# Attention with the value products directly behind a burst of scores

## The chip, the cores and the metric

The kernel runs on one core of one Trainium2 chip. The metric is the device time of one execution, in microseconds (us). Three executions of the kernel before took 730.85, 731.18 and 731.60 us; the median is 731.18 us.

## The reference, cut to what matters

The program is one layer of an encoder with 1024 tokens of 1024 features in float32: RMS norm, one input projection, three token mixers, output projection with residual, then RMS norm and a mixture of 32 experts, and a last norm. The change concerns two of the mixers, the attentions:

```python
def neighbourhood_attention(q, k, v, rel_bias):      # 4 heads of 64
    s = jnp.einsum('bhcd,bhrcjd->bhcrj', q_r, k_r).astype(jnp.float32) + bias
    p = jax.nn.softmax(s.reshape(B, H, GRID_W, kr * NA_COLS), axis=-1)
    return jnp.einsum('bhcrj,bhrcjd->bhcd', p, v_r)
...
def sliding_window_gqa(q, k, v, sink):               # 8 query heads, 2 key/value heads
    s = jnp.einsum('bnqgrd,bnkgd->bngrqk', qb, kb).astype(jnp.float32)
    s = jnp.where(jnp.asarray(valid)[None, :, None, None], s + alibi, -jnp.inf)
    p = jax.nn.softmax(jnp.concatenate([s, sink_logit], axis=-1), axis=-1)[..., :-1].astype(v.dtype)
    o = jnp.einsum('bngrqk,bnkgd->bnqgrd', p, vb)
```

Each query block of 128 tokens looks at its own key block and the ones before and after it: 384 keys, or 256 for the first and the last block.

## The kernel before, in words

The attention stage lies between the input projection and the output projection. It has 24 steps, made by `attention_plan` (line 89 on). Steps 0 to 7 are the neighbourhood attention of one query block each, with four heads. Steps 8 to 23 are the sliding-window attention, two steps for each query block, one for each key/value head (g = 0, then g = 1), with four query heads in each. So every step has four units u = 4s to 4s+3, one for each head, and 96 units in all.

What happens to a unit:

- TensorE multiplies query and key into one of four PSUM banks (`scores`, lines 801 to 816). The bank is u modulo 4, so the score of unit u waits until the evaluation of unit u-4 is done (`bias_done`).
- DVE evaluates the bank (`bias_and_max`, line 1505): it adds bias or distance, takes the row's extreme and writes the unit to SBUF. Line 1514 is the neighbourhood form, line 1526 the sliding-window form; the latter has a small copy of the sink in front of each step's first unit (line 1523).
- ACT takes the exponential and the row sum (line 1177). DVE takes the reciprocal of the sum two units later (line 1533). The normalisation is DVE's for some units (line 1550) and POOL's for the others (line 2039).

When all four units of a step are normalised, TensorE transposes them in chunks of 128 keys, four transposes to a chunk (`transposes`, line 829). A step has three chunks, or two at the edges. There are three PSUM banks for chunks, and DVE or ACT copies each to SBUF (`evacuate_chunk`, lines 485 and 490), by a rule that goes by the chunk's number. The value products (`times_values`, line 847 for the neighbourhood, line 853 for the sliding window) use the copied chunks. In the sliding window they come once for two steps, since the products of both key/value heads fill one bank. ACT copies that bank out (line 1190).

The order is written out by the plan as a list of ticks. Tick u carries the scores' units: at each u that is a multiple of four TensorE issues all four scores of a step as a burst, and then what the tick lists. An entry T is one chunk's transposes, an entry V one chunk's value products. The softmax of a step runs 8 ticks ahead of its first chunk (`lag = 8`), so that the chunks of step s begin in tick 4s+11, one tick in front of the scores of step s+3.

DVE and ACT walk through the same ticks in order. In each tick DVE does the evaluation of unit u, the reciprocal and, where it is DVE's, the normalisation of unit u-2, and then the evacuations of this tick's T entries that are its own. From tick 98 on it also splits the first output weights. ACT does the exponential of unit u, the copy of a finished value bank whose last V stood in the tick before, and then its own evacuations of the tick. An instruction that waits holds up all that is behind it on its engine. POOL only normalises, unit by unit.

In the plan before, a step's list is: its three T, then the V of the step before (where there is one), spread evenly over four ticks. For a step with three chunks and a V of three this gives T T | T | V V | V, and the burst of scores opens the second of these four ticks, so that TensorE runs: T, T, scores, T, V, V, V. For a sliding-window step without a V it is T | T | T.

After the last value products the output projection begins (lines 891 to 893), and later the experts, whose weights SyncE fetches as products release their buffers.

Of the kernel before, what the change touches and what calls it, by code (L numbers as in the profile page):

```python
# [61 lines left out]
MAGIC = 12582912.0  # L62

MIX_FROM = 8
GROUP = 3
LAST_QUERIES = (4, 8)
SLOPES = tuple(2.0 ** -(h + 1) for h in range(SWA_HEADS))
POOL_LAG = 2
# [20 lines left out]
def attention_plan():  # L89


    steps = []
    for i in range(TT):
        lo, hi = max(i - 1, 0), min(i + 2, TT)
        steps.append(("na", i, 0, lo * P, (hi - lo) * P))
    for b in range(TT):
        lo, hi = max(b - 1, 0), min(b + 2, TT)
        for g in range(SWA_KV):
            steps.append(("swa", b, g, lo * P, (hi - lo) * P))
    lag = 8  # L100
    ticks = [[] for _ in range(4 * len(steps) + lag + 4)]
    late = []
    for s, (kind, i, g, k0, nk) in enumerate(steps):
        nc_ = -(-nk // P)
        items = []
        for c0 in range(0, nc_, GROUP):
            group = range(c0, min(c0 + GROUP, nc_))
            items += [("T", s, c) for c in group]
            items += late
            late = [("V", s, c) for c in group] if kind == "na" or g == 1 else []  # L110
        if s == len(steps) - 1:
            items += late
        for j, it in enumerate(items):
            ticks[4 * s + 3 + lag + (4 * j) // len(items)].append(it)
    return steps, ticks


def encoder(nc, x, norm1_g, w_in, nat_tab, swa_sink, pool_w, pool_scale, w_out, norm2_g,
            rg_w, rg_b, re_w, re_b, e_gate, e_up, e_down, final_g,
            c_sq, c_namask, c_alibi, c_iedge, c_misc, c_dest, out):  # L120
    steps, ticks = attention_plan()
    NU = 4 * len(steps)

# [2062 lines left out]
```

How the kernel before makes its waits and increments, by code:

```python
        def chunk_ready(eng, n):  # L408
            if n >= 0:
                mine = by_vector(n)
                eng.wait_ge(pt_v if mine else pt_a, sum(by_vector(m) == mine for m in range(n + 1)))
# [63 lines left out]
        def evacuate_chunk(eng, copy, done, s, c):  # L476
            n = chunk_no[(s, c)]
            kind, i, g, k0, nk = steps[s]
            w = min(P, nk - c * P)
            eng.wait_ge(tr_done, n + 1)
            if kind == "na":
                if s >= 2:
                    eng.wait_ge(pv_done, vnum[(s - 2, last_chunk[s - 2])] + 1)
                copy(ptna[s % 2][0:w, c, :], ps[0:w, tbank(n), :]).then_inc(done, 1)
            else:
                before = NA_STEPS - 2 + i if i < 2 else NA_STEPS + 2 * (i - 2) + 1
                eng.wait_ge(pv_done, vnum[(before, last_chunk[before])] + 1)
                copy(ptswa[i % 2][c][:, g, :], ps[:, tbank(n), :]).then_inc(done, 1)
# [2 lines left out]
        @block.sync  # L493
# [1 line left out]
            def load_x(t):  # L495
                if t >= NX:
                    sp.wait_ge(x_in[t % NX], 16)
                sp.dma_start(xin[t][:], x[0, t * P:(t + 1) * P, :]).then_inc(x_in[t % NX], 16)
# [1 line left out]
            def load_w(i):  # L500
                m = ORDER[i]
                if i >= 2:
                    sp.wait_ge(w_split, 2 * (i - 1))
                sp.dma_start(wraw[i % 2][:], w_in[0, :, m * P:(m + 1) * P].rearrange("(k p) n -> p k n", p=P)
                             ).then_inc(w_in_s[i % 2], 16)
# [101 lines left out]
            sp.wait_ge(out_mm, TT)
            fetch_expert(0)
```

## Time and profile before

| | us |
|---|---|
| median of three runs | 731.18 |
| the profiled execution | 730.85 |
| its span, first to last instruction | 729.0 |
| TensorE busy in the span | 704.2 |
| VectorE (DVE) busy | 508.0 |
| ScalarE (ACT) busy | 390.1 |
| GpSimd (POOL) busy | 321.8 |

The span's times count from the first instruction. A busy TensorE is modelled from its pipelined matmuls, so the idle time in front of its weight loads (PEld) says more. A float32 transpose or matmul shows as two records, so a chunk of four transposes has eight, and the trace may group or miss some of them. Scores of two heads run side by side on the two halves of the array's rows, and the two key/value heads' products on the two halves of its columns, which is why their records come in pairs with the same start.

### The profile page before, as it was taken

Reading aid. Unit: us, or ns where it says so; the run is one execution under the profiler, and the core shown is the slowest. Engines: PE = TensorE matmul, PEld = TensorE weight load, DVE = VectorE, ACT = ScalarE, POOL = GpSimd, SP = SyncE. Lnnn points to the kernel's source line nnn. Section 1 sums busy time; section 2 is a strip of 40 time slices with the busy share of each in tenths; the row PEclk is TensorE's granted clock in tenths of the full one; section 3 lists DMA queues with packets and bytes.
Section 4 is the critical chain, followed back from the end, with each engine's and each line's share of the span. In section 5 each row is a group of like instructions: output and inputs, shape, how many; then the busy total and the mean of one; then the engine's idle time right before and its main releaser. Section 6 shows DMA issues by size and latency. Waiting matters only on the chain.

```text
span 729.0 us, 10252 instructions
## 1 busy us (share of the span) xinstructions
PE 704.2 (97%) x3757; PEld 511.3 (70%) x3757; DVE 508.0 (70%) x811; ACT 390.1 (54%) x585; POOL 321.8 (44%) x241
## 2 busy tenths in 40 slices
PE   7999999999999999999999899999999999999983
PEld 6888888886775556888889666666666666666631
DVE  5646422215988887214377898888888888888977
ACT  6500000104888887001122688888888888887815
POOL 2423458953778771610000454444444444442213
PEclk9999999999999999999999999999999999999997
DMA  9422112100400003705666599999999999999978
GB/s 308 140 58 58 32 55 59 30 0 23 123 1 1 1 1 140 206 5 200 230 227 207 178 351 385 390 384 381 383 383 384 390 383 383 385 386 379 400 273 350
DMA packets 62419, 157.74 MB, mean 216 GB/s; under 512 B 10168, under 2 KB 24992, under 8 KB 62368
## 3 DMA queue, kind: packets, MB, share of 16 engines
q1 hardware_dynamic: 55728, 139.58, 52.9%
q0 software_dynamic: 6336, 16.89, 7.0%
q8 instruction: 31, 0.51, 0.3%
q10 hardware_dynamic: 304, 0.59, 0.2%
q14 instruction: 20, 0.16, 0.1%
HBM read 142.36 MB, written 18.87 MB: 221 GB/s over the span
## 4 chain that ended last, share of the span: by engine, by line
PE 88%; DMA 5%; DVE 3%; SPq 1%; issue 1%; ACT 1%; POOL 0%; DVEq 0%; POOLq 0%
PE ps L1008 7%; PE ps L1013 7%; PE ps L1016 7%; PE ps L727 6%; PE ps L725 6%; PE ps L726 6%; PE ps L829 4%; PE ps L891 4%; PE ps L893 4%; PE ps L892 4%; PE ps L1039 4%; PE ps L1043 4%; PE ps L1035 4%; PE ps L814 3%; DMA wd<-in_expert_w_down 3%; PE ps L853 3%
## 5 line engine op out<-in xcount | busy, mean ns | idle before, releaser
L1810 DVE TENSOR_TENSOR wgulo<-wgu,unit 128x2048 fp32r<-128x2048 f32 x64 | 146.2, 2286 | 26.4 <-ACT unit L1276 26.4
L1276 ACT CAST unit<-wgu 128x2048 fp32r<-128x2048 f32 x64 | 122.2, 1910 | 3.7 <-PE ps L949 1.6
L2084 POOL DMA_INDIRECT expert_rows<-ysb,idx x32 | 70.8, 2212 | 108.2 <-ACT ysb L1323 107.2
L2077 POOL DMA_INDIRECT xg<-h_rows,idx x32 | 59.2, 1849 | 71.2 <-PE ps L984 58.3
L725 PE MATMUL ps<-hThi,whi 128*128 128x512 f32 x200 | 78.3, 392 | 0.0
L727 PE MATMUL ps<-hThi,wlo 128*128 128x512 f32 x200 | 77.9, 389 | 0.0
L726 PE MATMUL ps<-hTlo,whi 128*128 128x512 f32 x200 | 77.8, 389 | 0.0
L1816 DVE TENSOR_TENSOR wdlo<-wd,unit 128x2048 fp32r<-128x2048 f32 x32 | 73.1, 2285 | 2.6 <-ACT unit L1285 2.5
L1008 PE MATMUL ps<-unit,xThi 128*80 128x512 f32 x256 | 70.9, 398 | 0.8 <-ACT xThi L1300 0.8
L1013 PE MATMUL ps<-unit,xTlo 128*80 128x512 f32 x256 | 69.2, 391 | 0.0
L1016 PE MATMUL ps<-wgulo,xThi 128*80 128x512 f32 x256 | 69.1, 391 | 0.0
L1285 ACT CAST unit<-wd 128x2048 fp32r<-128x2048 f32 x32 | 61.1, 1909 | 4.8 <-DMA wd<-in_expert_w_down 4.8
L2039 POOL TENSOR_SCALAR pswa<-pswa,esum 128x384 f32<-128x384 f32 (+1 forms) x48 | 55.9, 1182 | 12.8 <-DVE esum L1533 12.8
L1137 ACT COPY kb<-ps 64x512 f32<-64x512 f32 x8 | 4.7, 583 | 92.6 <-DVE ps L1410 92.5
L1013 PEld LDWEIGHTS ps<-unit,xTlo 128*80 128x80 f32 x256 | 37.8, 148 | 21.1 <-DVE xTlo L1823 0.2
L1016 PEld LDWEIGHTS ps<-wgulo,xThi 128*80 128x80 f32 x256 | 37.8, 148 | 21.1
L891 PE MATMUL ps<-wohi,oThi 128*128 128x512 f32 x128 | 51.3, 401 | 0.0
L893 PE MATMUL ps<-wohi,oTlo 128*128 128x512 f32 x128 | 50.0, 391 | 0.0
L892 PE MATMUL ps<-wolo,oThi 128*128 128x512 f32 x128 | 49.9, 390 | 0.0
L1008 PEld LDWEIGHTS ps<-unit,xThi 128*80 128x80 f32 x256 | 35.4, 149 | 16.7 <-ACT xThi L1300 0.9
L1177 ACT ACTIVATE pswa<-pswa,mneg 128x385 f32<-128x385 f32 (+1 forms) x64 | 37.6, 588 | 13.0 <-DVE mneg L1526 12.8
L1972 POOL TENSOR_SCALAR stat<-stat 128x1 f32<-128x1 f32 x16 | 5.5, 344 | 87.8 <-ACT h L1249 65.3
(226 smaller groups left out, 1449.4 us busy)
## 6 DMA issues: line engine op xcount, KB each, us to landing
wgu<-in_expert_w_gate SPq DMA_DIRECT2D x64, 512.0 KB, 12.4
wgu<-in_expert_w_up SPq DMA_DIRECT2D x64, 512.0 KB, 15.3
wd<-in_expert_w_down SPq DMA_DIRECT2D x32, 1024.0 KB, 17.5
y<-expert_rows SPq DMA_DIRECT2D x16, 512.0 KB, 9.8
wraw<-in_w_in SPq DMA_DIRECT2D x14, 512.0 KB, 3.9
xin<-in_x SPq DMA_DIRECT2D x8, 512.0 KB, 6.7
x<-in_x SPq DMA_DIRECT2D x8, 512.0 KB, 7.3
out<-fo SPq DMA_DIRECT2D x8, 512.0 KB, 3.3
```

Source lines behind the costliest of these rows:

```text
L725: nc.tensor.matmul(bank, whi[i % 2][:, k, :], hThi[:, k, cols], start=(k == 0), stop=False)
L726: nc.tensor.matmul(bank, whi[i % 2][:, k, :], hTlo[:, k, cols], start=False, stop=False)
L727: mm = nc.tensor.matmul(bank, wlo[i % 2][:, k, :], hThi[:, k, cols], start=False, stop=(k == KT - 1))
L891: nc.tensor.matmul(ps[:, g % 4, :], oThi[t][:, k, :], wohi[n][:, k, :], start=(k == 0), stop=False)
L892: nc.tensor.matmul(ps[:, g % 4, :], oThi[t][:, k, :], wolo[n][:, k, :], start=False, stop=False)
L893: mm = nc.tensor.matmul(ps[:, g % 4, :], oTlo[t][:, k, :], wohi[n][:, k, :], start=False, stop=(k == KT - 1))
L1008: nc.tensor.matmul(bank, xThi[e % 2][:, 4 * a + k, :], hi[:, :, k * DE:(k + 1) * DE], start=(a == 0 and k == 0), stop=False)
L1013: nc.tensor.matmul(bank, xTlo[e % 2][:, 4 * a + k, :], hi[:, :, k * DE:(k + 1) * DE], start=False, stop=False)
L1016: mm = nc.tensor.matmul(bank, xThi[e % 2][:, 4 * a + k, :], lo[:, :, k * DE:(k + 1) * DE], start=False, stop=(a == 1 and k == 3))
L1276: nc.scalar.copy(weight_unit(e, a)[:], raw_half(wgu, e, a)).then_inc(ahi_done, 1)
L1810: nc.vector.tensor_tensor(raw_half(wgulo, e, a), raw_half(wgu, e, a), weight_unit(e, a)[:].bitcast(F32), ALU.subtract).then_inc(alo_done, 1)
L1816: nc.vector.tensor_tensor(wdlo[e % RING][:].rearrange("p j d -> p (j d)").rearrange("p (a f) -> p a f", a=2), wd[e % RING][:].rearrange("p ...
```

## The change

The plan no longer spreads a step's list evenly. With first = 4s+11, a step's chunks stand in ticks first, first+2 and first+3, and the V of the step before stands as a whole in tick first+1, the tick of a burst of scores. TensorE then runs: T, scores, V, V, V, T, T. The constant `GROUP`, which was 3 and so never split a step's chunks, is gone. The numbers of the chunks, and with them their banks and the engine that evacuates each, stay as they were, and so do the waits.

```diff
-        items = []
-        for c0 in range(0, nc_, GROUP):
-            group = range(c0, min(c0 + GROUP, nc_))
-            items += [("T", s, c) for c in group]
-            items += late
-            late = [("V", s, c) for c in group] if kind == "na" or g == 1 else []
+        first = 4 * s + 3 + lag
+        ticks[first + 1] += late
+        for c in range(nc_):
+            ticks[first + (0, 2, 3)[c]].append(("T", s, c))
+        late = [("V", s, c) for c in range(nc_)] if kind == "na" or g == 1 else []
         if s == len(steps) - 1:
-            items += late
-        for j, it in enumerate(items):
-            ticks[4 * s + 3 + lag + (4 * j) // len(items)].append(it)
+            ticks[first + 3] += late
```

## Rows read from the trace of the kernel before

**Rows 1.** The page's first line.
```profile
span 729.0 us, 10252 instructions
```
**Rows 2.** Table by stretch: length, busy time of each engine, granted clock, DMA share, GB/s.
```profile
178.40:283.00 104.60, 103.68 (x707) 61.54 (x705) 88.18 (x344) 83.55 (x238) 76.41 (x65) 1.00 0.09 26
...
400.00:700.00 300.00, 295.52 (x1540) 198.70 (x1539) 267.50 (x225) 240.06 (x226) 129.04 (x63) 1.00 0.99 367
393.00:397.00 4.00, 4.00 (x29) 4.00 (x29) 3.23 (x18) 2.44 (x2) 0.00 (x0) 0.57 0.98 379
```
**Rows 3.** TensorE's weight loads in order of time, neighbourhood steps: start, us, what.
```profile
185.73 0.42 PEld L829 LDWEIGHTS ps<-ident,pna 128*128 128x128 f32 x4 [0.55 <-issue]
...
188.37 0.95 PEld L809 LDWEIGHTS ps<-ka,qa 64*128 64x128 f32 x8 [0.17 <-issue]
189.86 0.42 PEld L829 LDWEIGHTS ps<-ident,pna 128*128 128x128 f32 x4 [0.54 <-DVE ptna L485]
190.45 1.29 PEld L847 LDWEIGHTS ps<-ptna,vtok 128*64 128x64 f32 x24 [0.17 <-issue]
191.91 0.86 PEld L829 LDWEIGHTS ps<-ident,pna 128*128 128x128 f32 x8 [0.17 <-POOL pna L2039]
192.93 0.95 PEld L809 LDWEIGHTS ps<-ka,qa 64*128 64x128 f32 x8 [0.17 <-issue]
...
211.38 1.29 PEld L847 LDWEIGHTS ps<-ptna,vtok 128*64 128x64 f32 x24 [0.55 <-issue]
```
**Rows 4.** DVE in order of time, neighbourhood steps.
```profile
192.60 0.69 DVE L485 COPY ptna<-ps 128x512 f32<-128x512 f32 x1 [0.16 <-PE ps L829]
193.88 0.56 DVE L1514 CUSTOM_DVE_ANT_0 pna<-ps,ti 128x384 f32<-128x384 f32 x1 [0.58 <-PE ps L809]
...
198.43 0.41 DVE L1514 CUSTOM_DVE_ANT_0 pna<-ps,te 128x256 f32<-128x256 f32 x1
```
**Rows 5.** TensorE's weight loads in order of time, one pair of sliding-window steps.
```profile
243.85 0.42 PEld L829 LDWEIGHTS ps<-ident,pswa 128*128 128x128 f32 x4 [0.81 <-POOL pswa L2039]
244.44 0.95 PEld L814 LDWEIGHTS ps<-kb,qs 64*128 64x128 f32 x8 [0.17 <-issue]
245.93 1.29 PEld L829 LDWEIGHTS ps<-ident,pswa 128*128 128x128 f32 x12 [0.55 <-issue]
...
247.99 0.30 PEld L814 LDWEIGHTS ps<-kb,qs 64*128 64x128 f32 x4 [0.17 <-DVE mneg L1526]
248.53 0.40 PEld L814 LDWEIGHTS ps<-kb,qs 64*128 64x128 f32 x2 [0.24 <-DVE mneg L1526]
249.13 0.29 PEld L814 LDWEIGHTS ps<-kb,qs 64*128 64x128 f32 x2 [0.20 <-DVE mneg L1526]
249.97 0.42 PEld L829 LDWEIGHTS ps<-ident,pswa 128*128 128x128 f32 x4 [0.54 <-issue]
250.56 0.20 PEld L853 LDWEIGHTS ps<-ptswa,vtok 128*64 128x64 f32 x4 [0.17 <-issue]
...
253.29 0.42 PEld L829 LDWEIGHTS ps<-ident,pswa 128*128 128x128 f32 x4 [0.81 <-POOL pswa L2039]
```
**Rows 6.** DVE in order of time, the same pair.
```profile
246.33 0.42 DVE L1550 TENSOR_SCALAR pswa<-pswa,esum 128x384 f32<-128x384 f32 x1
...
247.87 0.60 DVE L1526 CUSTOM_DVE_ANT_0 pswa<-ps,dist,nsink 128x384 f32<-128x384 f32 x1
...
248.47 0.60 DVE L1526 CUSTOM_DVE_ANT_0 pswa<-ps,dist,nsink 128x384 f32<-128x384 f32 x1
...
251.25 0.70 DVE L1550 TENSOR_SCALAR pswa<-pswa,esum 128x384 f32<-128x384 f32 x1
```
**Rows 7.** TensorE's weight loads, the end of the attention stage.
```profile
281.11 0.20 PEld L853 LDWEIGHTS ps<-ptswa,vtok 128*64 128x64 f32 x4 [0.48 <-ACT ptswa L490]
...
282.97 0.19 PEld L891 LDWEIGHTS ps<-wohi,oThi 128*128 128x128 f32 x1 [0.81 <-issue]
```
**Rows 8.** The chain of waits in order of time, expert stage.
```profile
647.99 21.75 DMA wd<-in_expert_w_down
```

More of the change, by code:

```diff
@@ L64 @@
 MIX_FROM = 8
-GROUP = 3
 LAST_QUERIES = (4, 8)
```

## The prediction

> **What bounds the kernel now.** I read the page first (span 729.0 us, [rows 1]), then the table by stage. In the attention stage, 178.4 to 283 us, TensorE is busy for 103.68 of 104.60 us, DVE for 88.18, and the DMA engines are almost idle; from 400 to 700 us the DMA share is 0.99 [rows 2]. TensorE's figure is modelled, so I went on to its weight loads in order of time, which show where it stands still, and to DVE in the same stretch. The chain of waits was read last, to see whether time lost in attention can be won back later.
>
> Names: S is a step's burst of four scores, T one transposed chunk (four transposes), V a step's value products. b is DVE's evaluation of one score bank, n its normalisation, ev the evacuation of a transposed chunk. Of the four scores in S, the first two wait for the first two b of the step before, the third for the third b, the fourth for the fourth.
>
> Neighbourhood steps: S starts at 188.37, T at 189.86 (1.49 us later), V at 190.45 (0.59), two T at 191.91 (1.46), next S at 192.93 (1.02) [rows 3]. A step is 4.56 us, nothing but TensorE's work. DVE is only slightly ahead: it stands 0.58 us before one b [rows 4].
>
> Sliding-window steps in pairs: T, S, four T, S, T, V, T, from 243.85 to 253.29, so 9.44 us: 0.59 + 1.49 + 2.06 + 1.98 + 0.59 + 2.73 [rows 5]. The first S runs freely in 1.49. The second does not: its third and fourth score wait for DVE (248.53 and 249.13), right behind the third and fourth b of the first S, which DVE finishes at 248.47 and 249.07 [rows 5, 6]. So in each pair TensorE is the bound, except in one burst, where DVE is.
>
> **What the change does to TensorE's own time.** No instruction is added or dropped, and no DMA is moved. A T between two other kinds takes 0.59, each further one in a row 0.43: two are 1.02 [rows 3], three 1.45. V behind S costs no more than V behind T: at 211.38 V follows 1.49 behind S and takes 1.46 [rows 3]. A neighbourhood step becomes 1.49 + 1.46 + 1.45 = 4.40, 0.16 less. A pair becomes, with its second S still at 1.98, 1.49 + 1.45 + 1.98 + 2.73 + 1.45 = 9.10, 0.34 less. If TensorE were alone, that would be the result.
>
> The trace's shapes change at each kind (scores 64*128, transposes 128*128, values 128*64), and the dearer first T is seen there. The Trainium skill, TensorEngine Tiling (Array Packing), Key Properties, says that changing the tiling mode drains the engine. By that rule fewer changes of kind mean a shorter stage; 0.16 us a change is what the rows show, and it is rival 1.
>
> **What it does to DVE.** DVE works in order. Its ev of a chunk stands in the tick where TensorE's T stands, behind that tick's b. In a step with V, the second T was before V, or before the burst; now it stands behind V, and its ev stands in front of the third b (a chunk that DVE takes as the step's third: in front of the fourth b). DVE therefore waits until S, V and T are over, with b's queued behind it for which the next S waits. DVE can begin ev 0.69 after the start of T (191.91 to 192.60) [rows 3, 4].
>
> A pair, with the start of its first S as 0. I take DVE's times from the row at 244.44. Steady state: T(s,1) behind V is at -1.45; its ev runs from -0.73 to -0.05; third and fourth b, 0.60 each [rows 6], end at 0.5 and 1.1. The third score starts at 0.57, the fourth at 1.17. A lone last score keeps TensorE for 0.84 (249.13 to 249.97) [rows 5], so T begins at 2.01 instead of 1.49. Three T last to 3.46, the second S starts. DVE goes on with the sink copy at 1.03, b to 1.87, n (0.42), b, ev (0.69), b to 4.11, b to 4.72: 0.1 later than now. The fourth score starts at 4.78, V at 5.62, T at 8.35, the next S at 9.80. I take 9.77 with the small overlaps of the rows: **+0.33 us a pair**. The T moved out of the half where TensorE waited for DVE anyway into the one where nothing is idle, and the free burst is now throttled too.
>
> Neighbourhood steps. b is 0.54 to 0.56, ev 0.69 [rows 4]. S4 still ends at 185.73 [rows 3]; V0 (1.02), three T and S5 follow, which starts at 188.20, 0.17 earlier than now. V1 starts at 189.92, T(2,1) at 191.38, its ev 192.1 to 192.8, third and fourth b to 193.76. S6 starts at 192.83, its fourth score at 193.82 instead of 193.36, V2 at 194.66. Laid out on in this way, the starts of S against now are: S6 -0.10, S7 +0.08, S8 +0.37, S9 +0.48, S10 +0.68 us. About +0.2 a step, where TensorE alone would give -0.16. The bursts of 256 columns (S7 to S9) have b of 0.41 [rows 4] to 0.48, which is in these numbers.
>
> Between the kinds: the chunk T(7,1) and then the first sliding chunks move behind V as well. Same method: S11 +1.31, S12 +1.15, S14 +1.68, S15 +1.13, S16 **+1.63**. Then three pairs to S22: +1.0. The last bursts and V19 have 256 columns and give back 0.4: V19 **+2.26**.
>
> Tail. Before, seven T stand behind V19; now nine, as T(20,1) and T(20,2) come behind it: 0.86. The pooled products wait for the last b, which is behind an ev: about 0.26. V23 waits now for ACT's ev of T(23,0) (0.48 before 281.11) and goes on to the output projection at 282.97 [rows 7]; that chain moves as it is. **+1.12**.
>
> ACT and POOL: ACT's copy of V's output now stands before the third exponential instead of behind the fourth, and waits for the end of V, 3.05 us into a neighbourhood step. The third b is at 4.1 or later in the steps where DVE waits, and its reciprocal comes two ticks on, so I take nothing. POOL's normalisations end 4 us before the T that needs them. Bounds: nothing to 0.3 us a step, over the five neighbourhood steps 0 to 1.5. DVE's n is 0.42 at 246.33 and 0.70 at 251.25 [rows 6]. The n in the path of the second S is the 0.42; should it come out as 0.70, a pair costs 0.28 more, over four pairs 1.1.
>
> Sum: 2.26 + 1.12 = **+3.4 us**. The profiled execution took 730.85 us, 1.85 around its span of 729.0; it would take 734.25. The median is 731.18, so **734.6**. Can it be won back? From 400 us the DMA engines are full, but their fetches are released by TensorE's products: the chain holds a 21.75 us transfer at 648 us that was issued behind TensorE's own work [rows 8]. The whole train starts later. TensorE's clock: from 393 to 397 us it was granted 0.57 on average, with the half level of 1.2 GHz in most of it, while the router's small products ran [rows 2]. Where that dip falls after a shift I can't say; its work takes 4 us, so at most half of it, and I allow 1 us either way.
>
> **Rivals.**
> 1. Faster: TensorE's changes of kind decide. 0.16 on six neighbourhood steps and 0.34 on six pairs, 3.0 us: 728.2. For it: TensorE is busy 99% of the stage. Against: the third and fourth score start 0.06 behind DVE's b already [rows 5, 6], and DVE has 88 of 104.6 us of work [rows 2] and would now stand over 1 us in each V step. It decides if ev behind V ends before the next S needs the third b, that is if DVE's wait were under 0.5 us. 9%.
> 2. Gains and waits cancel: the first free steps gain 0.16 each, the tail's waits are covered by output work: about +1 us, 732.2. 7%.
> 3. The later stages swallow it, since the expert stage is DMA bound: 731.2. Against: [rows 8], fetches are released by products. 4%.
> 4. More than that: ACT's early copy delays exponentials, or n takes 0.70. 2.6 us on top: 737.2. 12%.
> 5. The forecast, 734.6, own range 732.7 to 736. 68%.
>
> What this kernel's measurement can tell from no change is about 0.2%, 1.5 us. Slower 80%, same 11%, faster 9%. The range for 8 in 10 is 731.5 to 737.0: from rival 3's edge, over rival 2, to nearly the whole of rival 4.
>
> **What the profile after would show.** In a pair: V directly behind the second S; DVE idle for about 1 us before ev of line 490, released by TensorE's line 829; both bursts broken into single scores released by DVE; a pair of 9.7 to 9.8. In the neighbourhood steps the same idle before line 485, steps of 4.6 to 4.8. First output projection at 286.3 instead of 282.97, with everything behind it moved by as much. I am wrong if bursts stay at 1.49 and pairs fall under 9.3 (rival 1), or if DVE's waits are there but the last burst isn't later, or if the shift is gone at 400 us (rival 3).

## The result, and the profile after

The changed kernel takes 737.46 us (median of five; 736.49 to 741.66) against 730.85 us before (median of five): ratio 1.0088, 95% interval 1.0068 to 1.0108. Run once more, beside other executions of before, it gave 1.0082 (1.0063 to 1.0101). The medians lie 6.6 us apart, and 5.8 in the second series (737.20 against 731.45); 3.4 were forecast, and 737.46 lies outside the range.

The profiled execution is the longest of the five, 741.66 us. The second profiled execution took 737.47, with a span of 735.6. Two lines of the page of the first:

```profile
span 739.8 us, 10252 instructions
...
PE 714.7 (97%) x3757; PEld 518.0 (70%) x3757; DVE 510.6 (69%) x811; ACT 390.1 (53%) x585; POOL 320.3 (43%) x241
```

From the first score to the first output projection before took 116.3 us (166.64 to 282.97). After it takes 122.23 in both profiled executions. The two differ behind it. Table by stretch (length, busy time of TensorE, its weight loads, DVE, ACT and POOL, granted clock, DMA share, GB/s), after and after run again:

```profile
179.70:290.20 110.50, 109.43 (x706) 64.94 (x704) 90.29 (x345) 83.76 (x238) 75.99 (x65) 1.00 0.08 25
...
400.00:407.00 7.00, 7.00 (x42) 7.00 (x42) 5.24 (x28) 3.22 (x3) 0.00 (x0) 0.52 0.78 297
```

```profile
178.50:289.00 110.50, 109.43 (x706) 64.94 (x704) 90.29 (x345) 83.81 (x238) 76.06 (x65) 1.00 0.10 25
399.00:406.00 7.00, 5.91 (x58) 5.71 (x58) 5.66 (x29) 3.02 (x3) 0.00 (x0) 1.00 0.75 280
```

The attention's part is the same work in the same time. But in the first execution TensorE had a clock of 0.52 from 400 to 407 us, the 1.2 GHz level for nearly all of it, in the second the full 2.4 GHz; before had it for half as long [rows 2]. So 5.9 us are the attention's, 0.8% as in both ratios. What lies behind the stage took 449.6 us in the first execution, 446.6 in the second and 446.0 before.

A neighbourhood step after, TensorE's weight loads and then DVE, to be held against [rows 3, 4] (lines are 4 lower than before: 805 scores, 843 values, 825 transposes, 481 copy, 1510 b):

```profile
191.33 1.29 PEld L843 LDWEIGHTS ps<-ptna,vtok 128*64 128x64 f32 x24 [0.55 <-issue]
192.79 1.29 PEld L825 LDWEIGHTS ps<-ident,pna 128*128 128x128 f32 x12 [0.17 <-issue]
194.25 0.30 PEld L805 LDWEIGHTS ps<-ka,qa 64*128 64x128 f32 x4 [0.17 <-issue]
194.70 0.83 PEld L805 LDWEIGHTS ps<-ka,qa 64*128 64x128 f32 x4 [0.15 <-DVE mneg L1510]
```

```profile
191.67 0.53 DVE L1510 CUSTOM_DVE_ANT_0 pna<-ps,ti 128x384 f32<-128x384 f32 x1
...
193.48 0.69 DVE L481 COPY ptna<-ps 128x512 f32<-128x512 f32 x1 [0.73 <-PE ps L825]
194.09 0.55 DVE L1510 CUSTOM_DVE_ANT_0 pna<-ps,ti 128x384 f32<-128x384 f32 x1
```

V is behind S, three T in a row, 1.46 each, as laid out. DVE has its second b by 192.2 and stands 0.73 us before the copy at 193.48, which is 0.69 behind T(s,1) at 192.79. The third and fourth b come behind it. The burst that began at 194.25 is broken at 194.70 by the third of them, and the next V starts at 196.08: 1.83 us for the burst instead of 1.49.

A pair of sliding-window steps after, against [rows 5, 6], TensorE and then DVE (486 copy, 1519 sink copy, 1522 b, 1546 n):

```profile
248.99 0.30 PEld L810 LDWEIGHTS ps<-kb,qs 64*128 64x128 f32 x4 [0.17 <-issue]
249.50 0.43 PEld L810 LDWEIGHTS ps<-kb,qs 64*128 64x128 f32 x2 [0.21 <-DVE mneg L1522]
250.10 0.29 PEld L810 LDWEIGHTS ps<-kb,qs 64*128 64x128 f32 x2 [0.17 <-DVE mneg L1522]
250.94 1.34 PEld L825 LDWEIGHTS ps<-ident,pswa 128*128 128x128 f32 x12 [0.55 <-issue]
252.45 0.30 PEld L810 LDWEIGHTS ps<-kb,qs 64*128 64x128 f32 x4 [0.17 <-issue]
253.41 0.29 PEld L810 LDWEIGHTS ps<-kb,qs 64*128 64x128 f32 x2 [0.67 <-DVE mneg L1522]
254.01 0.29 PEld L810 LDWEIGHTS ps<-kb,qs 64*128 64x128 f32 x2 [0.31 <-DVE mneg L1522]
254.85 0.20 PEld L849 LDWEIGHTS ps<-ptswa,vtok 128*64 128x64 f32 x4 [0.55 <-ACT ptswa L486]
...
259.04 0.30 PEld L810 LDWEIGHTS ps<-kb,qs 64*128 64x128 f32 x4 [0.17 <-issue]
```

```profile
248.22 0.69 DVE L486 COPY ptswa<-ps 128x512 f32<-128x512 f32 x1 [2.05 <-PE ps L825]
248.83 0.61 DVE L1522 CUSTOM_DVE_ANT_0 pswa<-ps,dist,nsink 128x384 f32<-128x384 f32 x1
...
250.04 0.18 DVE L1519 COPY pswa<-nsink 128x4 f32<-128x4 f32 x1
...
250.99 0.64 DVE L1546 TENSOR_SCALAR pswa<-pswa,esum 128x384 f32<-128x384 f32 x1
...
252.16 0.67 DVE L486 COPY ptswa<-ps 128x512 f32<-128x512 f32 x1
```

And POOL, first after, then before:

```profile
249.62 2.46 POOL L2035 TENSOR_SCALAR pswa<-pswa,esum 128x384 f32<-128x384 f32 x2 [2.34 <-DVE esum L1529]
```

```profile
248.05 5.01 POOL L2039 TENSOR_SCALAR pswa<-pswa,esum 128x384 f32<-128x384 f32 x4 [1.98 <-DVE esum L1533]
```

The pair takes 10.05 us (248.99 to 259.04), before 9.44. Its first burst now waits twice too (0.21 and 0.17 in front of scores, 1.95 us instead of 1.49). The second waits 0.67 and 0.31 and takes 2.40 instead of 1.98. And n at 250.99 took 0.64 us: it started 0.15 us into the second of POOL's two instructions (250.84). Before, n ran at 246.33 for 0.42 us, and POOL stood idle from 246.07 to 248.05.

The same in sums. Groups of DVE instructions over the stage, after and then before (busy time, mean ns | idle before them, released by):

```profile
L486 DVE COPY ptswa<-ps 128x512 f32<-128x512 f32 x14 | 9.5, 680 | 12.6 <-PE ps L825 12.6
...
L1546 DVE TENSOR_SCALAR pswa<-pswa,esum 128x384 f32<-128x384 f32 x12 | 8.0, 663 | 0.4
...
L481 DVE COPY ptna<-ps 128x512 f32<-128x512 f32 x11 | 7.5, 683 | 4.5 <-PE ps L825 4.5
```

```profile
L490 DVE COPY ptswa<-ps 128x512 f32<-128x512 f32 x14 | 9.5, 675 | 0.9 <-PE ps L829 0.9
...
L485 DVE COPY ptna<-ps 128x512 f32<-128x512 f32 x11 | 7.5, 684 | 1.8 <-PE ps L829 1.6
L1550 DVE TENSOR_SCALAR pswa<-pswa,esum 128x384 f32<-128x384 f32 x12 | 6.8, 569 | 0.4
```

DVE stood idle for 17.1 us in front of its copies, before for 2.7 (2.05 of it in front of the copy at 248.22, where about 1 was forecast). The copies themselves did not grow; n did, from 569 to 663 ns.

The end of the stage, against [rows 7], and the transfer that answers to [rows 8]:

```profile
288.37 0.20 PEld L849 LDWEIGHTS ps<-ptswa,vtok 128*64 128x64 f32 x4 [0.47 <-ACT ptswa L486]
...
290.24 0.19 PEld L887 LDWEIGHTS ps<-wohi,oThi 128*128 128x128 f32 x1 [0.81 <-issue]
```

```profile
657.23 21.58 DMA wd<-in_expert_w_down
```

ACT's copy holds V23 for 0.47 us as before, the output projection starts at 290.24, 1.87 behind V23 (1.86 before), and the chain of waits crosses the same transfer 9.24 us later (21.58 us long). Nothing is won back. In the whole stage after, the trace names POOL as releaser of one weight load of TensorE (179.76), with no more than the usual 0.54 us in front of it.

### The profile page after: what moved, and what is told of

Read it like the earlier page. It is cut to its first block, busy times and chain, and to the rows that moved or that the text cites. A ratio compares the mean times of both kernels' runs of the same rounds, so it can differ in the third digit from the quotient of the medians.

```text
span 739.8 us, 10252 instructions
## 1 busy us (share of the span) xinstructions
PE 714.7 (97%) x3757; PEld 518.0 (70%) x3757; DVE 510.6 (69%) x811; ACT 390.1 (53%) x585; POOL 320.3 (43%) x241
## 4 chain that ended last, share of the span: by engine, by line
PE 85%; DMA 6%; DVE 5%; SPq 1%; issue 1%; ACT 1%; POOLq 0%; POOL 0%; DVEq 0%
PE ps L1004 7%; PE ps L1009 7%; PE ps L1012 7%; PE ps L723 6%; PE ps L722 6%; PE ps L721 6%; PE ps L887 4%; PE ps L889 4%; PE ps L888 4%; PE ps L1035 4%; PE ps L1039 4%; PE ps L1031 4%; DMA wd<-in_expert_w_down 3%; PE ps L810 3%; PE ps L849 3%; PE ps L825 3%
## 5 line engine op out<-in xcount | busy, mean ns | idle before, releaser
L1272 ACT CAST unit<-wgu 128x2048 fp32r<-128x2048 f32 x64 | 122.2, 1910 | 4.4 <-PE ps L945 2.2
```

The source lines that it names most:

```text
L1272: nc.scalar.copy(weight_unit(e, a)[:], raw_half(wgu, e, a)).then_inc(ahi_done, 1)
```

## The experiments

All times of a stage are from the first score to the first output projection, in that kernel's profiled execution. A pair is from one step's burst to the burst two steps on, the mean over S16 to S22; S22 is the start of step 22's burst, counted from the first score.

| kernel | neighbourhood step | pair | S22 | stage | median, ratio to before |
|---|---|---|---|---|---|
| before | 4.42 | 9.44 | 96.67 | 116.34 | 730.85 to 731.68 in four series |
| after | 4.61 | 10.05 | 101.08 | 122.23 | 737.46, 1.0088 |
| again | 4.61 | 10.05 | 101.08 | 122.23 | 737.20, 1.0082 |
| late_copy | 4.27 | 9.36 | 96.30 | 115.71 | 730.90, 0.9995 |
| copies_alone | 4.42 | 9.54 | 96.99 | 116.89 | 732.42 (one) |
| one_behind | 4.57 | 9.36 | 97.35 | 116.21 | 731.06, 0.9987 |
| short_pool | 4.61 | 9.81 | 99.38 | 120.15 | 735.08 (one; it leaves work out) |
| norm_first | 4.61 | 9.55 | 98.83 | 119.40 | 734.39 (one) |
| late_norm | 4.27 | 8.66 | 93.01 | 112.02 | 726.82, 0.9950 |
| before_norm | 4.42 | 9.40 | 96.59 | 116.06 | 731.04, 0.9999 |
| window_only | 4.42 | 10.05 | 99.03 | 120.18 | 734.87 (one) |
| neighbour_only | 4.61 | 9.43 | 98.71 | 118.36 | 735.09 (one) |
| old_tail | 4.61 | 10.05 | 101.08 | 121.49 | 736.77 (one) |
| copies_norm | 4.42 | 9.07 | 95.47 | 114.75 | 731.02 (one) |

The neighbourhood step is the mean over S5 to S8, narrow bursts included. Each kernel's steps are read from one trace; the two traces of the change agree in every burst to 0.01 us.

**late_copy: is it DVE's wait?** In DVE's loop, on top of the change:

```diff
+                due = [(s, c) for s, c in held if u >= 4 * s + 15]
+                held = [x for x in held if x not in due]
                 for kind, s, c in tick:
                     if kind == "T" and by_vector(chunk_no[(s, c)]):
-                        evacuate_chunk(dve, nc.vector.tensor_copy, pt_v, s, c)
+                        (held if c and s < 21 else due).append((s, c))
+                for s, c in due:
+                    evacuate_chunk(dve, nc.vector.tensor_copy, pt_v, s, c)
```

> The changed kernel with one difference: DVE's copies of a step's second and third chunk stand behind the fourth b of the next burst instead of in front of the third or fourth. TensorE's order is that of the change. Theory A (DVE waits in its queue for the transposes behind V, with the b's behind it): bursts run freely again, neighbourhood steps 4.40 us, pairs of sliding-window steps 9.1 to 9.3 instead of 10.05, attention stage (first score to first output projection) 114 to 115 us instead of 122.2 after and 116.3 before, total about 729. Theory B (the order S, V, T itself costs on TensorE, whatever DVE does): pairs stay at 9.8 or more, total 736 to 738.

Stage 115.71, pair 9.36, ratio 0.9995 (0.9981 to 1.0009). With TensorE's order untouched, 6.5 of the 122.2 us went, more than the change had cost. Theory A holds and theory B falls: V directly behind S costs nothing on TensorE. The neighbourhood steps went to 4.27, under before's 4.42, and a full-width one (S5 to S6) took 4.41 where before took 4.57: the 0.16 of the changes of kind. The pair missed the expected 9.1 to 9.3, and with it the stage the 114 to 115 and the total the 729. TensorE's loads and DVE in it:

```profile
244.70 0.95 PEld L810 LDWEIGHTS ps<-kb,qs 64*128 64x128 f32 x8 [0.17 <-issue]
...
247.65 0.48 PEld L810 LDWEIGHTS ps<-kb,qs 64*128 64x128 f32 x4 [0.17 <-issue]
248.44 0.29 PEld L810 LDWEIGHTS ps<-kb,qs 64*128 64x128 f32 x2 [0.30 <-DVE mneg L1522]
249.03 0.29 PEld L810 LDWEIGHTS ps<-kb,qs 64*128 64x128 f32 x2 [0.30 <-DVE mneg L1522]
249.87 0.20 PEld L849 LDWEIGHTS ps<-ptswa,vtok 128*64 128x64 f32 x4 [0.55 <-ACT ptswa L486]
...
254.06 0.95 PEld L810 LDWEIGHTS ps<-kb,qs 64*128 64x128 f32 x8 [0.17 <-issue]
```

```profile
243.94 0.69 DVE L486 COPY ptswa<-ps 128x512 f32<-128x512 f32 x1 [0.24 <-PE ps L825]
245.65 0.41 DVE L1519 COPY pswa<-nsink 128x4 f32<-128x4 f32 x1 [1.02 <-PE ps L810]
...
246.83 0.42 DVE L1547 TENSOR_SCALAR pswa<-pswa,esum 128x384 f32<-128x384 f32 x1
```

The copy now meets a transpose that is nearly done (0.24 us of wait) and holds up no b. The first burst is free. The second still waits for the third and fourth b. Their chain is one sink copy of 0.41 us, an n and four b long, and the runs short_pool, norm_first and late_norm ask what stretches that chain.

**copies_alone: or the copy's place in the queue?** TensorE and ACT keep the plan before; DVE walks through a second list with the chunks in the changed ticks:

```diff
+    moved = [[] for _ in ticks]
+    for u, tick in enumerate(ticks):
+        for kind, s, c in tick:
+            if kind == "T":
+                moved[4 * s + 3 + lag + (0, 2, 3)[c]].append((kind, s, c))
...
-            for u, tick in enumerate(ticks):
+            for u, tick in enumerate(moved):
```

> The kernel before with one difference: DVE makes its copies in the ticks of the changed plan, TensorE and ACT keep the plan before. So DVE's queue is in the order of the change, but no transpose stands behind V more than before. Theory A (the wait for the transposes costs, not the place of the copy in DVE's queue): pairs 9.4 to 9.5, attention stage 116 to 117 us. Rival (a copy in front of the third b costs by its 0.69 us of work alone): pairs 9.9 or more, stage over 119.

Pair 9.54 (0.04 over what was expected), stage 116.89: +0.55 of the 5.89. A copy in front of the third b is cheap as long as its chunk is there. It is the wait that costs, not the 0.69 us.

**one_behind: only the third chunk behind V.**

```diff
-            ticks[first + (0, 2, 3)[c]].append(("T", s, c))
+            ticks[first + (0, 0, 2)[c]].append(("T", s, c))
```

> The changed kernel with the second chunk in front of the burst again: T T, burst, V, T, so only the third chunk stands behind V. V is directly behind S as in the change, and three T still stand in a row. In the sliding window it is the second chunk that DVE copies. Theory A: DVE has no wait behind V there, pairs 9.1 to 9.3 us; neighbourhood steps 4.4 to 4.7, as every second one has a third chunk that DVE copies; stage 114 to 116 us, total 729 to 731. Theory B (V directly behind S costs): pairs 9.8 or more, total over 735.

Pair 9.36, neighbourhood step 4.57, stage 116.21, ratio 0.9987 (0.9977 to 0.9997). As A has it, except that the pair is again 9.36 and not under 9.3: the same as in late_copy, with the same chain of b behind the first burst, and that the stage lies 0.2 over the 116. Where DVE copies third chunks, in the neighbourhood, the step stayed long.

**short_pool: what stretches n?**

```diff
-                    gp.tensor_scalar(pbuf(u), pbuf(u), esum[:, u:u + 1], None, ALU.mult).then_inc(norm_p, 1)
+                    gp.tensor_scalar(pbuf(u)[:, 0:64], pbuf(u)[:, 0:64], esum[:, u:u + 1], None, ALU.mult).then_inc(norm_p, 1)
...
-                nc.scalar.copy(dst, src).then_inc(o_out, 1)
+                nc.scalar.mul(dst, src, 1.0 / 384).then_inc(o_out, 1)
```

> The changed kernel with POOL normalising only the first 64 columns of its units, and the value bank scaled by 1/384 when it is copied out to keep the numbers small; so most of POOL's normalisation is left out, and only the attention stage is to be read. It tests theory C: DVE's normalisation and its sink copy last longer when they meet a POOL operation (0.59 to 0.70 instead of 0.42), and the one in the free half of the pair lies on the path. C: this normalisation 0.42, pairs 9.75 to 9.85 instead of 10.05, stage about 120.5 instead of 122.2. Rival (POOL has no part in it): pairs 10.05, stage 122.

Pair 9.81, stage 120.15, as expected. DVE and TensorE in a pair:

```profile
246.12 0.69 DVE L486 COPY ptswa<-ps 128x512 f32<-128x512 f32 x1 [2.38 <-PE ps L825]
...
248.86 0.42 DVE L1546 TENSOR_SCALAR pswa<-pswa,esum 128x384 f32<-128x384 f32 x1
```

```profile
246.88 0.30 PEld L810 LDWEIGHTS ps<-kb,qs 64*128 64x128 f32 x4 [0.17 <-issue]
...
251.06 0.29 PEld L810 LDWEIGHTS ps<-kb,qs 64*128 64x128 f32 x2 [0.42 <-DVE mneg L1522]
```

n is 0.42 instead of 0.64 and the third score of the second burst starts 4.18 behind the first burst (246.88 to 251.06), where it was 4.42 (248.99 to 253.41). TensorE's transposes don't wait for POOL, yet POOL's work costs 2.08 us of the stage, through DVE. The kernel before was not run with POOL's work cut, so these 2.08 us are what that work costs after the change; that before loses none of it is shown only for the n in the pairs (0.42, [rows 6]).

**norm_first: is n on the path with its whole length?**

```diff
-            return u % 8 in ((1, 3, 6) if u < 4 * NA_STEPS else (3, 6))
+            return u % 8 in ((1, 3, 6) if u < 4 * NA_STEPS else (2, 3))
```

> The changed kernel with DVE's two normalisations of a sliding-window pair both in the step with V (units with u%8 = 2 and 3 instead of 3 and 6), so that none lies between the first and the second b of the step without V; POOL takes the unit with u%8 = 6. If the stretched normalisation lies on the path with its whole 0.64 us, the pair falls from 10.05 to 9.4 or 9.5, the stage from 122.2 to about 119. Rival (the path runs through the transposes behind V and the normalisation only fills idle time): pairs 10.0, stage 122.

Pair 9.55, stage 119.40. The expected 9.4 to 9.5 was missed by a little; 0.50 of n's 0.64 us were on the path, as far as the move changed nothing else. This n now stands in the step with V, where DVE waits for transposes anyway.

**late_norm: both obstacles taken away.** late_copy with the second n of a pair moved into the step with V:

```diff
-            return u % 8 in ((1, 3, 6) if u < 4 * NA_STEPS else (3, 6))
+            return u % 8 in ((1, 3, 6) if u < 4 * NA_STEPS else (3, 5))
```

> late_copy (DVE's copies behind the fourth b) and DVE's second normalisation of a sliding-window pair moved out of the step without V (u%8 = 5 instead of 6). In late_copy the second burst still waits for the fourth b, which ends 4.27 us after the first burst's start, with 0.42 us of normalisation in that chain. Expected: fourth b at 3.8, pairs 8.9 instead of 9.36, stage 113 instead of 115.7, total 728 to 729. Rival (POOL, with five units in a row, or ACT becomes the bound): pairs over 9.2.

726.82 us, ratio 0.9950 (0.9932 to 0.9967), the fastest kernel of this case: 0.5% under before and 10 us under the change. Pair 8.66, better than the 8.9 expected. TensorE and DVE:

```profile
233.74 0.95 PEld L810 LDWEIGHTS ps<-kb,qs 64*128 64x128 f32 x8 [0.17 <-issue]
235.23 1.29 PEld L825 LDWEIGHTS ps<-ident,pswa 128*128 128x128 f32 x12 [0.54 <-issue]
236.69 0.98 PEld L810 LDWEIGHTS ps<-kb,qs 64*128 64x128 f32 x8 [0.17 <-issue]
238.21 0.20 PEld L849 LDWEIGHTS ps<-ptswa,vtok 128*64 128x64 f32 x4 [0.54 <-ACT ptswa L486]
...
240.94 1.29 PEld L825 LDWEIGHTS ps<-ident,pswa 128*128 128x128 f32 x12 [0.81 <-issue]
242.40 0.95 PEld L810 LDWEIGHTS ps<-kb,qs 64*128 64x128 f32 x8 [0.17 <-issue]
```

```profile
234.69 0.17 DVE L1519 COPY pswa<-nsink 128x4 f32<-128x4 f32 x1 [0.72 <-PE ps L810]
...
241.40 0.64 DVE L1547 TENSOR_SCALAR pswa<-pswa,esum 128x384 f32<-128x384 f32 x1
```

Both bursts are free now (1.49, and 1.52 from 236.69 to 238.21); the sum of TensorE's pieces is 1.49 + 1.46 + 1.49 + 2.73 + 1.46 = 8.63. My 8.9 had left a lone fourth score; b ends early enough that scores still go in twos, and the sink copy came out at 0.17, not 0.41.

**before_norm: the same move in the old order.** The same line in the kernel before.

> The kernel before with the same move of the normalisation alone (u%8 = 5 instead of 6). In its order DVE's copy of the chunk that follows the first burst stands behind the first b and can't begin before 2.2 us after the burst's start, which is where the normalisation ends now. So the gap is filled by waiting: pairs 9.4, stage 116, total within 0.1% of before. Rival (the normalisation's 0.42 us count wherever it stands): pairs 9.0, stage 114, total 729.

Pair 9.40, stage 116.06, ratio 0.9999 (0.9988 to 1.0009), as expected. Where DVE's next instruction waits for a transpose, a shorter queue in front of it is worth nothing. **copies_norm**, copies_alone with that line, lets the second b go first:

> copies_alone (TensorE by the plan before, DVE's copies in the ticks of the change) and the normalisation moved as in late_norm. It asks what TensorE's old order gives when DVE is out of its way as far as that order lets it. b's chain without the normalisation and the copy before the second b: fourth b about 4.3 us after the first burst instead of 4.63: pairs 9.1 to 9.2, stage 114.5 to 115. Rival (the order of TensorE has no part in late_norm's gain): pairs 8.7, stage 112.

Pair 9.07 (0.03 under the expected), stage 114.75, as expected. With TensorE's old order that is the best of these runs, with the order of the change it is 112.02. The two kernels differ in the place of DVE's copies too, so not all of the 2.73 us between them is shown to be TensorE's order.

**window_only, neighbour_only, old_tail: where the cost arises.** The plan before under a condition, `kind == "na"`, `kind == "swa"` and `s >= 20`:

```diff
+        if kind == "na":
+            items = []
+            for c0 in range(0, nc_, 3):
...
+        else:
             first = 4 * s + 3 + lag
             ticks[first + 1] += late
```

> The new plan for the sliding-window steps 8 to 23 only, the plan before for the neighbourhood steps. By the traces of before and after, the change cost 0.4 us up to the eighth burst, 1.3 to the twelfth, 2.6 to the sixteenth, 4.4 to the twenty-second, 5.9 at the end. If the parts are independent: stage about 121.5, that is 5.2 of the 5.9 us. Rival (DVE's lateness is handed on from the neighbourhood steps): stage under 120.5.

> The new plan for the neighbourhood steps 0 to 7 only, the plan before for the sliding-window steps. The new plan in the window alone cost 3.84 us of the stage's 5.89. If the rest, 2.05 us, is the neighbourhood's own and stays to the end: stage 118.4. If it is handed on only by the changed plan behind it (DVE's lateness is worked off in the pairs of the old plan, where DVE has 1.7 us idle in each): 1.3 us or less, stage 117.6 or less.

> The changed kernel with the plan before for steps 20 to 23 only. From the twenty-second burst to the output projection before took 19.66 us, the change 21.15. If the two more chunks behind V and the last b's that stand behind a copy make the tail: this stretch 19.6 to 20.0, stage about 120.8. Rival (the tail is late because DVE comes late into it): still over 20.8.

window_only's stage is 120.18 (+3.84), neighbour_only's 118.36 (+2.02). The sum is 5.86 of 5.89, so the parts are independent. My figure of 121.5 for the first was wrong all the same, and by its number alone the rival (under 120.5) would have stood; neighbour_only is what decides. I had read the split off the place where the delay appears. The neighbourhood's change costs 0.43 us up to S8, 1.43 at S12 and 2.05 at S14, as its last chunks lie between the first sliding steps. old_tail took 20.41 us from S22 to the output projection (19.66 before, 21.15 after), between the expected 19.6 to 20.0 and the rival's 20.8: the order of steps 20 to 23 is half of the tail's 1.49 us, where I had thought it all. In late_copy TensorE has the change's order to the end, and DVE has the change's places for the copies of steps 21 to 23; only those up to step 20 stand later. There the same stretch takes 19.41 us. So with these copies out of the way the whole of the tail's loss goes; whether the other half comes from step 20's copies or from DVE's lateness on the way in isn't separated.

**again: the change once more.**

> The changed kernel once more, unchanged. Its stage was 5.9 us longer and its median 6.6 us above before; its profiled execution had a stretch of 6.8 us at half clock near 400 us, the one of before 3.4. If the 0.7 us are the clock's and not the change's: ratio near 1.008, stage 122.2, and an execution without that stretch lies about 5.9 us above one of before without it. Rival: the changed kernel is always 6.6 us or more above, with a second place of loss behind the stage.

Ratio 1.0082 and stage 122.23, as expected. The span, 735.6, lies 6.6 above before's. This execution had no stretch at half clock near 400 us, and before's had one, so less than 5.9 was to be expected, and I was wrong: 0.55 of the 6.6 lie behind the output projection's start. Over all kernels here that part took 445.2 to 449.6 us. The clock does not account for the whole of that: after had half clock for 15.6 us of its span and took 449.6, copies_norm had it for as long and took 446.7. A second place of loss isn't shown, and a small one isn't excluded.

## Why the prediction was right and where it was wrong

Right was the direction and the mechanism: DVE's copy waits behind V with the b's behind it (17.1 us of wait against 2.7), both bursts of a pair are throttled, nothing is won back later, and rivals 1, 2 and 3 fall. Rival 1 falls doubly, since late_copy shows its saving to be real (4.27 a step) and lost by the wait alone. TensorE's pieces V and T (1.46, 1.45, 2.73) were right to 0.01. Against before, in us, counted from the first score, the starts of:

| | S6 | S8 | S10 | S12 | S16 | S22 | V19 | output projection |
|---|---|---|---|---|---|---|---|---|
| predicted | -0.10 | +0.37 | +0.68 | +1.15 | +1.63 | +2.6 | +2.26 | +3.4 |
| measured | -0.07 | +0.43 | +0.80 | +1.28 | +2.56 | +4.41 | +4.41 | +5.89 |

The neighbourhood part is right within 0.13 us up to S12. What failed is the length of DVE's small instructions in the sliding window, the term "b to 1.87, n (0.42), b". n measured 0.64 in the free half of a pair, and the fourth b of that half ended 4.96 behind the burst instead of 4.72; the pair came out at 10.05 instead of 9.77. I had the term as a bound, "should it come out as 0.70, a pair costs 0.28 more", and took the wrong end of it, because I went by the instruction's place in the kernel before. In the row I chose POOL was idle; after the change POOL was at work there. The excess by stretches:

- S16 to S22: +1.85 instead of +1.0. With POOL's work cut, short_pool has +1.12 (S22 less S16: 29.42, before 28.30). That is 0.73 of the 0.85 too much.
- S12 to S16: +1.28 instead of +0.48. In short_pool +0.31, and its S16 lies at +1.59 where +1.63 was forecast. The same cause: DVE's n took 0.59 and 0.63 (at 218.97 and 222.31) and a sink copy 0.42 (at 217.19), in short_pool 0.42, 0.42 and 0.17.
- S22 to V19: nothing came back, where I had 0.4. In short_pool 0.38 came back.
- Tail, V19 to the output projection: +1.48 instead of +1.12. In short_pool it is +1.48 too, so these 0.36 us are not POOL's, and they are not explained.

Of the 2.51 us between 3.38 and 5.89, short_pool accounts for 2.08, as far as before would not gain by the same cut. One more size was off: DVE's wait behind V was put at about 1 us and measured 2.05. The pair as I had laid it out would have given about 2 (the fourth b at 4.72, ev at 9.07, and 2.28 of work between them by the rows after); I hadn't taken the wait from it, and the sum doesn't use it. The range failed with n: it held rival 4, n at 0.70, for four pairs only and not for the steps between the kinds, and it ended at 737.0 where the median came out at 737.46. Rival 4's other half, ACT's early copy, did not show: late_norm has that copy and runs at TensorE's pace.

## What to carry to other kernels

When an order of one engine is moved, look in every other engine's queue for the instruction that follows the moved one, and for what stands behind it: a cheap copy in a strict queue costs the whole wait. Moving it behind what is urgent took back the loss of 0.8% (late_copy), and moving the normalisation out of the chain as well gave 0.5% over the kernel before (late_norm). Take the duration of an instruction from a row in which its neighbours on other engines do what they will do after the change, not from the row in the same place of the program.

## What the runs showed of the hardware

DVE's n (128 x 384 float32, in SBUF) lasts 0.42 us alone. Beside a POOL normalisation of 384 columns (1.24 us) its length goes in these traces by when it starts in POOL's. POOL's spans in a profile are rough, but the same offsets come back in every trace. Started 0.15 us into it 0.64, at 0.20 0.59, at 0.27 0.52, from 0.39 to 0.54 0.42, at 0.75 0.70 to 0.71, at 0.82 0.63 to 0.65, at 1.02 0.44. So it ends about 0.79 us after POOL's start, or 0.21 after POOL's end, whichever is the next, and where it would end between the two without a wait (started at 0.39 to 0.54) it isn't held at all. The sink copy of four columns, 0.15 to 0.17 us alone, goes the same way, with an end 0.60 behind POOL's start (0.43 at 0.17) or 0.03 behind POOL's end (0.41 at 0.86). POOL waits too: where an n reaches into the start of its next instruction, that one lasts 1.34 us instead of 1.24 (251.72 in the kernel before). The Trainium skill, GPSIMD Engine Reference, section Specifications, lists the SBUF interfaces as shared with VectorE, with contention for DVE instructions in a two-port mode or with two SBUF inputs. That n is such an instruction no run here shows; that the two engines hold each other up these rows show.

Two float32 scores on the two halves of the array's rows ran side by side where both were released together: a burst is 1.49 us in twos. Released one behind the other, 0.60 us apart, they ran singly, and a lone last score of 384 columns keeps TensorE for 0.84 us from its weight load. In the first burst of the pair after, the third and fourth came so (249.50 and 250.10), and the burst took 1.95 us, 0.46 more.
